# A two-layer diffusion backbone on one core: the MLPs' second product by seven quadrant products instead of eight

## The chip, the cores and the metric

The kernel runs on one core of a Trainium2 chip. The metric is the device time of one execution in microseconds (us). TensorE (PE in the profile) multiplies, ScalarE is ACT, VectorE is DVE, GpSimd is POOL, and SyncE (SP) issues the loads.

## The reference, cut to what matters

1024 sample tokens and 256 prompt tokens go through two layers with shared weights. Each layer is a mixer followed by an MLP; the change is mostly in the MLPs.

```
x = x + g1 * out                                   # mixer: layer 0 gMLP and retention, layer 1 pooling
h = _rms_norm(x, norm_mlp[i]) * (1.0 + sc2) + sh2
x = x + g2 * (jnp.square(jax.nn.relu(h @ mlp_w1[i])) @ mlp_w2[i])
```

The model width is 1024 and the hidden width 4096. In layer 0 a retention mixer also needs the running states of two scan directions at each of ten blocks of 128 tokens, and returns the prompt's final states.

## The kernel before, in words

All values are float32. For accuracy each operand of a product is kept as two tiles in a reduced format, a high part and the remainder (names ending in H and L), and each product is three matmuls: high x high, high x low, low x high (`pair_pass`, where nearly all matmuls have line L314). The high part is made by a copy on ScalarE, the low part by a subtraction: on GpSimd for weights (`split_lo`), on VectorE for the hidden values (`hidden_lo`).

Everything is transposed: the features are on the 128 partitions and the tokens run along the free axis in three blocks `TB`: two of 512 sample tokens, one of 256 prompt tokens. The sum `X` (8 tiles of features by 1280 tokens) stays in SBUF.

Each MLP runs over NCH = 16 chunks of 256 hidden features. One chunk has these steps:

- First product: six groups (three token blocks by two tiles of 128 hidden features), each of 8 x 3 = 24 matmuls, into PSUM banks 0 and 1 in turn.
- For each group: relu on ScalarE (L774), square on VectorE (L1336), high part on ScalarE into `midH` (L767), low part on VectorE into `midL` (L1329).
- Second product: 24 groups (three token blocks by eight tiles of output features), each of 2 x 3 = 6 matmuls, into banks 2 to 5 in turn. VectorE adds each one, times the gate, into `X` (L1061, called an eviction below). TensorE may use a bank again when the eviction four groups back is done.
- Weights: SP loads 1 MB of W1 or W2 into `stage`, ScalarE makes `ringH` (L532, `split_hi`), GpSimd makes `ringL` (L854, `split_lo`). There is one `stage`, and a ring of two slots: one holds W1 and one W2. W1 of the next chunk is split as soon as the last first-product group has been issued, W2 of this chunk when the chunk before is over.

The order on each engine is written out by hand, and semaphores (counts of finished steps) tie the engines together. Chunks 1 to 14 are a hardware loop with one body per engine, for each of the two layers. Layer 0's chunks carry extra work for layer 1's modulation: `ada_part` on VectorE in four parts of four instructions, and `ada_of_chunk` on TensorE.

The retention stage of layer 0 spills the states to DRAM and then reads them back block by block (`state_loads`), into two buffers per direction, `S[d][k % 2]`. The prompt's final states also lie in `S[d][0]`, and must have been written out before block 0 can be loaded there. GpSimd computes tables for the pooling mixer (`bandT`, `bandM` and others) just behind chunk 0 of layer 0.

## Time and profile before

| what | value |
|---|---|
| median of 3 runs | 2645.57 us (2644.88 to 2650.03) |
| the profiled execution | 2645.16 us, of which 2643.4 us are the profiled span |
| TensorE matmul busy | 2561.9 us, 97% of the span |
| VectorE busy | 1351.4 us, 51% |
| ScalarE busy | 593.9 us, 22% |
| GpSimd busy | 544.8 us, 21% |
| DMA | mean 75 GB/s |
| matmuls of the two MLPs | most of the rows of L314, which hold 83% of the chain that ended last |

A matmul's row is longer than the time in which it keeps the next one waiting, since matmuls are pipelined: what counts for TensorE is the distance from one start to the next. The same holds a little for VectorE and ScalarE, whose next instruction starts shortly before the row of the last one ends.

### The profile page before, as it was taken

What the parts mean: (1) busy time and instruction counts of PE and PEld (TensorE: products, weight loads), DVE (VectorE), ACT (ScalarE), POOL (GpSimd) and SP (SyncE); (2) the same over time, 40 slices, a digit from 0 to 9 for tenths busy, and PEclk for the clock granted to TensorE, in tenths of its full rate; (3) what the DMA queues carried; (4) which work ended last, traced back from release to release, by engine and by line L of the source; (5) the groups of instructions that cost most, each with busy time, mean ns of one, the idle gap of its engine ahead of it and who ended that gap; (6) DMA issues with size and microseconds to landing.
All of it is one profiled execution on the core that took longest, in us unless ns stands there. A gap on an engine that the chain in (4) does not pass through costs nothing.

```text
span 2643.4 us, 37530 instructions
## 1 busy us (share of the span) xinstructions
PE 2561.9 (97%) x14604; PEld 2240.7 (85%) x14604; DVE 1351.4 (51%) x2366; ACT 593.9 (22%) x982; POOL 544.8 (21%) x230
## 2 busy tenths in 40 slices
PE   7899999979999999999999999999999999999998
PEld 3878899977888888888888888888888888888887
DVE  6635752264385556554556555564444444444445
ACT  3311122142231111111111112751112111121112
POOL 6124321162121212111112111011121211212110
PEclk9999999989999999999999999899999999999999
DMA  7314523274212211211211211011010100101102
GB/s 236 149 67 142 166 96 112 95 265 168 72 33 80 71 56 56 95 56 56 71 56 56 95 56 32 25 32 33 32 48 32 48 32 32 48 32 48 32 32 80
DMA packets 126263, 199.48 MB, mean 75 GB/s; under 512 B 4420, under 2 KB 102504, under 8 KB 125800
## 3 DMA queue, kind: packets, MB, share of 16 engines
q1 hardware_dynamic: 123216, 188.76, 21.1%
q10 hardware_dynamic: 2968, 9.63, 1.2%
q8 instruction: 55, 0.90, 0.1%
q14 instruction: 24, 0.20, 0.0%
HBM read 167.44 MB, written 26.74 MB: 73 GB/s over the span
## 4 chain that ended last, share of the span: by engine, by line
PE 88%; DVE 5%; issue 2%; DMA 2%; ACT 2%; POOL 1%; ACTq 0%; SPq 0%; DVEq 0%; POOLq 0%
PE bank L314 83%; PE bank L1404 1%; PE bank L1432 1%; PE bank L1557 1%; DMA ada_st_in<-in_ada_w_dram 1%; PE bank L1469 1%; DVE ada_acc_in L1053 0%; PE bank L1735 0%; DVE vtok L1107 0%; DMA SB<-state_spill 0%; DVE xgm L1220 0%; POOL ringL L854 0%; DVE h1L L1227 0%; DVE X L1061 0%; ACT pF L736 0%
## 5 line engine op out<-in xcount | busy, mean ns | idle before, releaser
L854 POOL TENSOR_TENSOR ringL<-stage,ringH 128x2048 fp32r<-128x2048 f32 x82 | 392.8, 4790 | 1823.1 <-ACT ringH L532 1823.1
L1061 DVE SCALAR_TENSOR_TENSOR X<-bank,mod,X 128x512 f32<-128x512 f32 (+1 forms) x792 | 515.1, 660 | 363.4 <-PE bank L314 359.1
L314 PE MATMUL bank<-midH,ringH 128*128 128x512 f32 (+1 forms) x1536 | 546.7, 356 | 3.3 <-DVE X L1061 3.3
L314 PE MATMUL bank<-midL,ringH 128*128 128x512 f32 (+1 forms) x1536 | 544.9, 355 | 0.0
L314 PE MATMUL bank<-midH,ringL 128*128 128x512 f32 (+1 forms) x1536 | 544.7, 355 | 0.0
L314 PE MATMUL bank<-hH,ringH 128*128 128x512 f32 (+1 forms) x1248 | 447.2, 358 | 0.2 <-DVE hL L1227 0.2
L314 PE MATMUL bank<-hH,ringL 128*128 128x512 f32 (+1 forms) x1248 | 442.5, 355 | 0.0
L314 PE MATMUL bank<-hL,ringH 128*128 128x512 f32 (+1 forms) x1248 | 442.4, 355 | 0.0
L1336 DVE TENSOR_TENSOR relu<-relu 128x512 f32<-128x512 f32 (+1 forms) x192 | 146.3, 763 | 568.9 <-ACT relu L774 568.8
L774 ACT ACTIVATE relu<-bank 128x512 f32<-128x512 f32 (+1 forms) x192 | 100.9, 527 | 1375.9 <-PE bank L314 1375.9
L314 PEld LDWEIGHTS bank<-midH,ringH 128*128 128x128 f32 x1536 | 291.5, 190 | 46.1 <-DVE X L1061 6.5
L314 PEld LDWEIGHTS bank<-midH,ringL 128*128 128x128 f32 x1536 | 291.2, 190 | 40.6
L314 PEld LDWEIGHTS bank<-midL,ringH 128*128 128x128 f32 x1536 | 291.7, 190 | 39.5
L314 PE MATMUL bank<-h1H,ringH 128*128 128x512 f32 (+1 forms) x768 | 272.4, 355 | 0.2 <-DVE h1L L1227 0.2
L314 PE MATMUL bank<-h1L,ringH 128*128 128x512 f32 (+1 forms) x768 | 271.8, 354 | 0.0
L314 PE MATMUL bank<-h1H,ringL 128*128 128x512 f32 (+1 forms) x768 | 271.6, 354 | 0.0
L314 PEld LDWEIGHTS bank<-hH,ringL 128*128 128x128 f32 x1248 | 236.6, 190 | 33.4
L314 PEld LDWEIGHTS bank<-hH,ringH 128*128 128x128 f32 x1248 | 236.9, 190 | 32.5 <-DVE hL L1227 1.0
L314 PEld LDWEIGHTS bank<-hL,ringH 128*128 128x128 f32 x1248 | 236.9, 190 | 31.5
L314 PE MATMUL bank<-ringH,hH 128*128 128x256 f32 x640 | 186.2, 291 | 13.7 <-DVE hL L1030 13.7
L314 PE MATMUL bank<-ringL,hH 128*128 128x256 f32 x640 | 183.3, 286 | 0.0
L314 PE MATMUL bank<-ringH,hL 128*128 128x256 f32 x640 | 183.1, 286 | 0.0
(191 smaller groups left out, 2888.1 us busy)
## 6 DMA issues: line engine op xcount, KB each, us to landing
stage<-in_mlp_w_dram SPq DMA_DIRECT2D x64, 1024.0 KB, 5.3
ada_st_mlp<-in_ada_w_dram SPq DMA_DIRECT2D x18, 1536.0 KB, 8.3
stage<-in_ev_w_in_dram SPq DMA_DIRECT2D x14, 1024.0 KB, 5.1
ada_st_in<-in_ada_w_dram SPq DMA_DIRECT2D x8, 1536.0 KB, 9.5
ada<-in_ada_w_dram SPq DMA_DIRECT2D x8, 1024.0 KB, 13.3
x_spill<-X SPq DMA_DIRECT2D x1, 5120.0 KB, 18.5
gate_spill<-gate_st ACTq DMA_DIRECT2D x8, 640.0 KB, 3.7
gt<-gate_spill SPq DMA_DIRECT2D x20, 256.0 KB, 3.3
```

The costliest lines, as they stand in the source:

```text
L314: mm = nc.tensor.matmul(out, a, b, start=first and n == 0, stop=last and n == 2)
L774: nc.scalar.activation(r_b[g % 3][:, 0:w], bank[g if first and g < 4 else g % 2][:, 0:w], ACT.Relu).then_inc(relu_ok[l], 1)
L854: nc.gpsimd.tensor_tensor(ringL[slot][:, :], stage[:, :], ringH[slot][:, :].bitcast(F32), ALU.subtract).then_inc(w_lo, 1)
L1061: V.scalar_tensor_tensor(out=X[:, d, cols(t)], in0=src[:, 0:TB[t][1]], scalar=gate_ap, in1=X[:, d, cols(t)], op0=ALU.mult, op1=ALU.add).th ...
L1336: V.tensor_tensor(r, r, r, ALU.mult).then_inc(sqr_ok[l], 1)
L1404: mm = nc.tensor.matmul(ADA_BANK[:, col(4 * j + 2 * i)], ada_acc[pr][:, j, i, :], ones[:, 0:2], start=True, stop=True)
L1432: mm = nc.tensor.matmul(bank[i // 2][0:2, UC * (i % 2):UC * (i % 2 + 1)], sc2[:, k, :], ada0[i][:, k, :], start=(k == 0), stop=(k == DT - 1))
L1469: mm = nc.tensor.matmul(bank[6 + d][:, h * P:(h + 1) * P], kx[j % 2][:, d, h, :], val[:, n, h * P:(h + 1) * P], start=True, stop=True)
L1557: mm = nc.tensor.transpose(tile_pair(q, j)[:, d * P:(d + 1) * P], X[:, d, n * P:(n + 1) * P], ident)
```

## The change

Three things change.

First, in chunks 1 to 14 of both layers the second product of the 1024 sample tokens is cut in quadrants: two halves of hidden features (A11, A12, A21, A22 are W2's quadrants) and two halves of tokens (B11, B12, B21, B22 are the hidden values'). Eight products of quadrants become seven, of sums S1 to S4 of weights and T1 to T4 of hidden values (the scheme of Strassen and Winograd). Products 1, 6, 7, 4 run on in one bank without clearing it, and 5 and 3 likewise, so each of the 28 results (seven products by four tiles) is added to one tile of `X`. The weight sums are made on GpSimd, the T sums on VectorE, and both are split in high and low parts. The eight prompt groups stay as they are. `mlp_fast` is the loop body on each engine.

Second, `state_loads` uses the other buffer, `S[d][(k + 1) % 2]`, so block 0's load no longer waits for the final states to have left; the wait for the last input product moves behind the second state loads, the gate loads and a weight load.

Third, the pooling tables are computed in layer 0's last chunk rather than behind its first. Some small tiles move (`r_b`, `fin`).

```diff
+FACTORS = {1: ("A11", "B11"), 2: ("A12", "B21"), 3: ("S4", "B22"), 4: ("A22", "T4"), 5: ("S1", "T1"), 6: ("S2", "T2"),
+           7: ("S3", "T3")}
+GOES_TO = {1: (0, 0), 2: (0, 0), 6: (0, 1), 5: (1, 1), 7: (1, 1), 3: (0, 1), 4: (1, 0)}
+CHAIN = {6: 1, 7: 6, 4: 7, 3: 5}
+FAST_SEQ = ([(1, d) for d in range(HD)] + [(2, d) for d in range(HD)]
+            + [(p, d) for d0 in range(0, HD, 2) for p in (6, 5, 7, 3, 4) for d in (d0, d0 + 1)] + [("prompt", d) for d in range(DT)])
+FAST_BANK = [(2, 3, 6, 1, 4, 5, 2, 3)[d] if p == "prompt" else (6, 1)[d % 2] if p in (2, 3, 5) else 2 + d for p, d in FAST_SEQ]
+LO_ORDER = ["B11", "B21", "T1", "T2", "T3", "B22", "T4", "p0", "p1"]
...
-        sp.wait_ge(in_mm, IN_CUM[N_IN])
-        sp.wait_ge(a_spilled[0], 16 * 2 * NTB * HT)
-        sp.wait_ge(a_spilled[1], 16 * 2 * NTB * HT)
-
...
-                sp.dma_start(S[d][k % 2][:, :, :].rearrange("p h e -> p (h e)"), s_dram[d][k]).then_inc(s_back[k % 2], 16)
+                sp.dma_start(S[d][(k + 1) % 2][:, :, :].rearrange("p h e -> p (h e)"), s_dram[d][k]).then_inc(s_back[k % 2], 16)
```

The end of the new body on ScalarE (the last line makes W1's high part):

```diff
+            relu(4, hidden("p0")[2])
+            square(4, hidden("p0")[2])
+            act.wait_ge(sqr_ok[l], n0 + 5)
+            high("p0")
+            relu(5, hidden("p1")[2])
+            square(5, hidden("p1")[2])
+            act.wait_ge(sqr_ok[l], n0 + 6)
+            high("p1")
+            split_hi(U + 2, (m1_mm[l], n0 + PAIRS), U_MLP[l] % 2)
```

The new body on GpSimd:

```diff
+        def mlp_fast(l, ch):
...
+            pool.wait_ge(w_raw, 16 * (U + 2))
+            pool.wait_ge(m2_mm[l], products(l, ch) - DT)
+            nc.gpsimd.tensor_tensor(s1, a21, a22, ALU.add).then_inc(s_add[l], 1)
+            nc.gpsimd.tensor_tensor(s3, a11, a21, ALU.subtract).then_inc(s_add[l], 1)
+            pool.wait_ge(s_add[l], 4 * ch - 3)
+            nc.gpsimd.tensor_tensor(s2, s1, a11, ALU.subtract).then_inc(s_add[l], 1)
+            pool.wait_ge(s_add[l], 4 * ch - 1)
+            nc.gpsimd.tensor_tensor(s4, a12, s2, ALU.subtract).then_inc(s_add[l], 1)
+            split_lo(U + 1, (U_MLP[l] + 1) % 2)
+            pool.wait_ge(s_hi[l], ch)
+            pool.wait_ge(t_full[l], 4 * ch - 3)
+            nc.gpsimd.tensor_tensor(sumL[:, :, :], sumF[:, :, :], sumH[:, :, :].bitcast(F32), ALU.subtract).then_inc(s_lo[l], 1)
+            split_lo(U + 2, U_MLP[l] % 2)
```

The new body on VectorE, where `evict(n)` is one eviction and `lower` makes a low part:

```diff
+        def mlp_fast(l, ch):
...
+            ada(0)
+            square(0)
+            lower("B11", b11)
+            ada(1)
+            square(1)
+            lower("B21", b21)
+            square(2)
+            dve.wait_ge(sqr_ok[l], n0 + 3)
+            V.tensor_tensor(t1, b12, b11, ALU.subtract).then_inc(t_full[l], 1)
+            for n in range(2 * HD):
+                evict(n)
+            ada(2)
+            ada(3)
+            dve.wait_ge(sqr_ok[l], n0 + 4)
...
+            for n in range(2 * HD, FAST_GRP):
+                evict(n)
+                if n in (11, 13):
+                    lower("p0" if n == 11 else "p1")
```

The new body on TensorE (each `second_product` first waits until the last eviction from its bank is done):

```diff
+        def mlp_fast(l, ch):
...
+            first_product(0)
+            pe.wait_ge(m2_ev[l], p0 - 4)
+            first_product(1)
+            pe.wait_ge(relu_ok[l], n0 + 1)
+            first_product(2)
+            pe.wait_ge(w_lo, UA + 2)
+            for n in range(HD):
+                second_product(n)
+            pe.wait_ge(relu_ok[l], n0 + 2)
+            for n in range(HD, 2 * HD):
+                second_product(n)
...
+            first_product(3)
+            pe.wait_ge(m2_ev[l], p0 + 2 * HD)
+            first_product(4)
+            pe.wait_ge(relu_ok[l], n0 + 4)
+            first_product(5)
+            pe.wait_ge(s_lo[l], ch)
+            pe.wait_ge(relu_ok[l], n0 + 5)
+            for n in range(2 * HD, 7 * HD):
+                second_product(n)
```

The body that GpSimd runs for each of chunks 1 to 14 of layer 1 was, before (`ringL_56` and `ringL_57` are the low parts of W2 and of the next chunk's W1):

```order
L986 ISA
L854 TENSOR_TENSOR ringL_56<-stage,ringH_54 128x2048 [waits w_hi]
L853 REGISTER_ALU
L854 TENSOR_TENSOR ringL_57<-stage,ringH_55 128x2048 [waits w_hi]
L986 REGISTER_ALU
L986 COMPARE_AND_BRANCH
```

and is now:

```order
L1096 TENSOR_TENSOR sumF<-stage 128x512 [waits m2_mm1]
L1097 TENSOR_TENSOR sumF<-stage 128x512
L1098 ISA
L1099 TENSOR_TENSOR sumF<-sumF,stage 128x512 [waits s_add1]
L1100 REGISTER_ALU
L1101 TENSOR_TENSOR sumF<-stage,sumF 128x512 [waits s_add1]
L967 TENSOR_TENSOR ringL_56<-stage,ringH_54 128x2048 [waits w_hi]
L1105 TENSOR_TENSOR sumL<-sumF,sumH 128x2048 [waits t_full1,s_hi1]
L966 REGISTER_ALU
L967 TENSOR_TENSOR ringL_57<-stage,ringH_55 128x2048 [waits w_hi]
```

Four sums stand ahead of the two splits, and the split of the sums stands between them. The last row, the next chunk's W1, stays last.

On VectorE, layer 1's body had all six low parts ahead of the first eviction; its rows at that place were, before:

```order
L1336 TENSOR_TENSOR relu_174<-relu_174 128x256 [waits relu_ok1]
L1329 TENSOR_TENSOR midL<-relu_173,midH 128x256 [waits mid_hi1]
L1329 TENSOR_TENSOR midL<-relu_174,midH 128x256 [waits mid_hi1]
L1058 ISA
L119 REGISTER_ALU [waits m2_mm1]
L1061 SCALAR_TENSOR_TENSOR X<-bank,mod,X 128x512 [waits m2_ev1]
```

and behind the low part of T4 (first row) it now has, where `bank1` is banks 2 and 3, `bank3` bank 6 and `bank0` bank 1:

```order
L1504 TENSOR_TENSOR ts4L_145<-relu0_178,ts4H_144 128x512 [waits mid_hi1]
L1194 REGISTER_ALU
L1197 SCALAR_TENSOR_TENSOR X_51<-bank1,mod_156,X_51 128x512 [waits m2_ev1,m2_mm1]
...
L1197 SCALAR_TENSOR_TENSOR X_51<-bank3,mod_156,X_51 128x512 [waits m2_ev1,m2_mm1]
L1197 SCALAR_TENSOR_TENSOR X_51<-bank0,mod_156,X_51 128x512 [waits m2_ev1,m2_mm1]
L1503 REGISTER_ALU
L1504 TENSOR_TENSOR midL_53<-midF_143,midH_52 128x256 [waits mid_hi1]
L1194 REGISTER_ALU
L1197 SCALAR_TENSOR_TENSOR X_51<-bank1,mod_156,X_51 128x512 [waits m2_ev1,m2_mm1]
```

The prompt's two low parts (rows with 128x256) have moved in between evictions: the first stands behind the fourth eviction of this phase and ahead of the fifth (that of product 7), the second two evictions later.

## Rows read from the trace of the kernel before

**Rows 1.** The page: span, busy time of TensorE's two parts and the others.

```profile
span 2643.4 us, 37530 instructions
PE 2561.9 (97%) x14604; PEld 2240.7 (85%) x14604; DVE 1351.4 (51%) x2366; ACT 593.9 (22%) x982; POOL 544.8 (21%) x230
```

**Rows 2.** Windows of one chunk: stretch, length, busy us by engine, granted clock, DMA.

```profile
1908.16:1963.24 55.08, 55.08 (x291) 47.55 (x290) 23.50 (x37) 9.58 (x14) 9.23 (x2) 1.00 0.12 38
...
1025.30:1081.80 56.50, 56.50 (x301) 48.81 (x300) 31.20 (x52) 9.58 (x14) 9.53 (x2) 1.00 0.19 65
```

**Rows 3.** Timeline of TensorE, layer 1: start, length, instruction (11 and 19 left out).

```profile
1850.17 0.28 PE L314 MATMUL bank<-midH,ringH 128*128 128x256 f32 x1
...
1852.57 0.28 PE L314 MATMUL bank<-midH,ringL 128*128 128x256 f32 x1
...
1855.12 0.39 PE L314 MATMUL bank<-h1H,ringH 128*128 128x512 f32 x1
...
1857.84 0.39 PE L314 MATMUL bank<-h1H,ringH 128*128 128x512 f32 x1
```

**Rows 4.** Timeline of ScalarE in one chunk of layer 1.

```profile
1968.95 0.60 ACT L774 ACTIVATE relu<-bank 128x512 f32<-128x512 f32 x1 [29.98 <-PE bank L314]
...
1990.95 0.38 ACT L774 ACTIVATE relu<-bank 128x256 f32<-128x256 f32 x1 [1.98 <-PE bank L314]
1991.23 0.41 ACT L767 ACTIVATE midH<-relu 128x256 fp32r<-128x256 f32 x1
1991.83 0.42 ACT L767 ACTIVATE midH<-relu 128x256 fp32r<-128x256 f32 x1 [0.19 <-DVE relu L1336]
1992.15 1.90 ACT L532 ACTIVATE ringH<-stage 128x2048 fp32r<-128x2048 f32 x1
```

**Rows 5.** Timeline of VectorE: square, eviction, five evictions in a row.

```profile
1914.51 0.69 DVE L1336 TENSOR_TENSOR relu<-relu 128x512 f32<-128x512 f32 x1 [5.69 <-ACT relu L774]
...
1940.07 0.75 DVE L1061 SCALAR_TENSOR_TENSOR X<-bank,mod,X 128x512 f32<-128x512 f32 x1 [0.61 <-PE bank L314]
...
1053.82 3.38 DVE L1061 SCALAR_TENSOR_TENSOR X<-bank,mod,X 128x512 f32<-128x512 f32 x5
```

**Rows 6.** Timelines of GpSimd and VectorE where they overlap.

```profile
1590.93 4.58 POOL L854 TENSOR_TENSOR ringL<-stage,ringH 128x2048 fp32r<-128x2048 f32 x1 [23.77 <-ACT ringH L532]
...
1591.97 3.82 DVE L1336 TENSOR_TENSOR relu<-relu 128x256 f32<-128x256 f32 x1 [2.46 <-ACT relu L774]
...
1589.09 0.42 DVE L1336 TENSOR_TENSOR relu<-relu 128x256 f32<-128x256 f32 x1 [2.81 <-ACT relu L774]
...
1939.05 4.62 POOL L854 TENSOR_TENSOR ringL<-stage,ringH 128x2048 fp32r<-128x2048 f32 x1 [18.08 <-ACT ringH L532]
...
1053.45 4.94 POOL L854 TENSOR_TENSOR ringL<-stage,ringH 128x2048 fp32r<-128x2048 f32 x1 [20.35 <-ACT ringH L532]
```

**Rows 7.** Timeline and windows: two stalls of TensorE and the stretches behind them.

```profile
1619.77 0.58 PE L314 MATMUL bank<-midH,ringH 128*128 128x256 f32 x1 [2.26 <-DVE X L1061]
...
1619.30:1622.60 3.30, 2.83 (x13) 2.83 (x14) 2.07 (x6) 0.00 (x0) 3.30 (x1) 0.51 0.01 2
...
563.00:568.00 5.00, 3.29 (x30) 3.10 (x30) 4.56 (x17) 3.37 (x10) 4.34 (x5) 1.00 0.65 190
```

**Rows 8.** Chain of waits and timeline at the start of the retention stage.

```profile
528.87 4.52 DMA out_dram<-SB
533.85 2.89 DMA SB<-state_spill
...
536.78 0.80 PE L1622 MATMUL bank<-val,pt 128*128 128x128 f32 x2 [5.86 <-DMA SB<-state_spill]
...
532.57 2.48 DVE L1175 TENSOR_TENSOR pt<-bank,tab 128x512 f32<-128x512 f32 x4 [11.49 <-DMA gate_spill<-gate_st]
```

**Rows 9.** Timeline of GpSimd: first and last table instruction, two 512-column products.

```profile
774.72 0.69 POOL L945 MEMSET bandT<- 128x144 f32 x4
...
785.25 0.10 POOL L972 MEMSET band_edge<- 128x1 f32 x1
...
542.60 2.49 POOL L919 TENSOR_TENSOR qd<-qk,tab 128x512 f32<-128x512 f32 x2 [9.11 <-PE bank L1623]
```

More of the change, by code:

```diff
@@ L221, in build @@
     ones = small("ones", [P, P])
-    r_b = [at(f"relu{i}", A_V + 2 * i, [P, 512]) for i in range(3)]
+    r_b = [at(f"relu{i}", A_AD + 3 + 2 * i, [P, 512]) for i in range(3)]
     acc = at("acc", A_E + 15, [P, T])
@@ L305, in cols, with pair_pass @@
         return slice(t0, t0 + w)
-    def pair_pass(out, w_hi_ap, w_lo_ap, m_hi_ap, m_lo_ap, first, last, weights_moving=False):
+    def pair_pass(out, w_hi_ap, w_lo_ap, m_hi_ap, m_lo_ap, first, last, weights_moving=False, chained=False):
         if weights_moving:
@@ L313, in pair_pass @@
         for n, (a, b) in enumerate(terms):
-            mm = nc.tensor.matmul(out, a, b, start=first and n == 0, stop=last and n == 2)
+            mm = nc.tensor.matmul(out, a, b, start=first and n == 0, stop=last and n == 2, skip_group_check=chained)
         return mm
@@ L348, in h_part, with hidden, weight @@
         return (hH, hL)[part][:, d, cols(tb)]
+    MID_PART = {"B11": (0, 0), "B21": (1, 0), "T1": (0, 1), "B22": (1, 1), "T2": (0, 0), "T3": (1, 0), "p0": (0, 2), "p1": (1, 2)}
+    def hidden(name):
+        if name == "T4":
+            return ts4H[:, :], ts4L[:, :], r_b[0][:, :]
+        k, tb = MID_PART[name]
+        return tuple(m[:, k, cols(tb)] for m in (midH, midL, midF))
+    def weight(l, name, d):
+        if name[0] == "S":
+            i = int(name[1]) - 1
+            return tuple(m[:, i, d * P:(d + 1) * P] for m in (sumH, sumL))
+        k, n0 = int(name[2]) - 1, HD * (int(name[1]) - 1)
+        return tuple(r[(U_MLP[l] + 1) % 2][:, k * D + (n0 + d) * P:k * D + (n0 + d + 1) * P] for r in (ringH, ringL))
     def slot_free(U):
@@ L477, in _ @@
         state_loads(0)
+        for d in range(2):
+            sp.dma_start(new_state[0, 0, d].rearrange("h d e -> d h e"), S[d][NT % 2][:, :, :]).then_inc(new_out, 16)
+        sp.wait_ge(new_out, 32)
         state_loads(1)
@@ L1357, in mlp, with square, lower, evict @@
                         finish(j)
+        def mlp_fast(l, ch):
+            n0, h0, p0 = PAIRS * ch, halves(l, ch), products(l, ch)
+            def square(g):
+                dve.wait_ge(relu_ok[l], n0 + g + 1)
+                V.tensor_tensor(r_b[g][:, :], r_b[g][:, :], r_b[g][:, :], ALU.mult).then_inc(sqr_ok[l], 1)
+            def lower(name, src=None):
+                hi, lo, full = hidden(name)
+                dve.wait_ge(mid_hi[l], h0 + LO_ORDER.index(name) + 1)
+                V.tensor_tensor(lo, full if src is None else src, hi.bitcast(F32), ALU.subtract).then_inc(mid_lo[l], 1)
+            def evict(n):
+                t, d = FAST_TILE[n]
+                own = earlier(FAST_TILE, n)
+                update(m2_mm[l], p0 + n + 1, m2_ev[l], bank[FAST_BANK[n]], mod[:, l, 5 * DT + d, TB[t][2]:TB[t][2] + 1], t, d,
+                       (m2_ev[l], p0 + own + 1))
+            def ada(part):
+                if l == 0:
+                    ada_part(BATCHES_L0 + ch, 1, part, 4)
+            b11, b21, b12 = (r[:, :] for r in r_b)
+            t1, t2, t3, t4, b22 = (hidden(name)[2] for name in ("T1", "T2", "T3", "T4", "B22"))
+            ada(0)
[12 more added lines that the diff above has]
+            dve.wait_ge(sqr_ok[l], n0 + 4)
+            dve.wait_ge(t_full[l], 4 * ch - 3)
+            V.tensor_tensor(t2, b22, t1, ALU.subtract).then_inc(t_full[l], 1)
+            V.tensor_tensor(t3, b22, b12, ALU.subtract).then_inc(t_full[l], 1)
+            dve.wait_ge(t_full[l], 4 * ch - 2)
+            V.tensor_tensor(t4, b21, t2, ALU.subtract).then_inc(t_full[l], 1)
+            lower("T1")
+            dve.wait_ge(t_full[l], 4 * ch)
+            lower("T2")
+            lower("T3")
+            lower("B22")
+            lower("T4")
+            for n in range(2 * HD, FAST_GRP):
+                evict(n)
+                if n in (11, 13):
+                    lower("p0" if n == 11 else "p1")
         mlp(0, 0, first=True)
@@ L1622, in _ @@
                         nc.tensor.matmul(out, pt[n % 2][:, d, h, :], val[:, n, h * P:(h + 1) * P], start=True, stop=False)
-                        mm = nc.tensor.matmul(out, qd[n % 2][:, d, h, :], S[d][n % 2][:, h, :], start=False, stop=True)
+                        mm = nc.tensor.matmul(out, qd[n % 2][:, d, h, :], S[d][(n + 1) % 2][:, h, :], start=False, stop=True)
                     mm.then_inc(y_mm, 1)
@@ L1658, in mlp @@
                     g = HT * nth + f
-                    after(pe, relu_ok[l], g - 3 if first else n0 + g - 1)
+                    after(pe, relu_ok[l], g - 3 if first else n0 + (max(g - 1, 0) if last else g - 1))
+                    if last and g == 1:
+                        pe.wait_ge(m2_ev[l], products(l, ch))
                     if first and g == HT:
```

214 lines of the change are left out of this document (156 added, 58 removed).

## The prediction

> **What bounds the kernel now.** I began with the page's busy times: TensorE is busy for 97% of the span, no other engine for more than 51% [rows 1]. The windows of single chunks sharpen that: in a chunk of layer 1 TensorE is busy for all of 55.08 us, in one of layer 0 for all of 56.50 us [rows 2]. A busy row is pipelined, so I took the distance between starts from the timeline: twelve 512-column matmuls lie between 1855.12 and 1857.84, or 0.2267 us each, and twenty 256-column ones between 1850.17 and 1852.57, or 0.12 us each [rows 3]. A chunk has 192 and 96 of them: 192 x 0.2267 + 96 x 0.12 = 55.04 us. So the MLP loops are bound by the sheer number of matmuls, and every other engine hides. The reader is to see both sides of this: each matmul taken out is worth its whole slot, and each wait put before TensorE costs its whole length.
>
> **What the change removes.** One product of eight, four tiles by three matmuls: 12 matmuls a chunk, 12 x 0.2267 = 2.72 us, in 28 chunks 76.2 us. That is all that can be won here. TensorE's own work per chunk of layer 1 falls to 52.32 us. (The page "TensorE: Matmul & The Clock Gate" of the Trainium skill, section "Back-to-back issue gap", would put a lone 512-column matmul's slot at about 216 ns; by that the saving would be 72.5 us. The trace has the duration, so the trace's is used.)
>
> **What it adds, step by step, for one chunk of layer 1.** C is the start of the chunk's first matmul. Durations: a group of the first product takes 24 slots, 5.44 us at 512 columns and 2.88 at 256; one tile of a quadrant product 3 slots, 0.68 us. An engine that waits for TensorE starts about 0.3 us after the last slot (a row is 0.39 long in a slot of 0.227, and the semaphore follows) [rows 3]. A relu or a high part takes 0.60 us, a VectorE operation of 512 columns from SBUF 0.69 (the next can start 0.61 after it) [rows 4, 5]. An eviction takes 0.75 alone; five in a row took 3.38, so each costs (3.38 - 0.75) / 4 = 0.66 when they queue [rows 5]. ScalarE's new squares I take like its copies.
>
> (a) *The first eight tiles.* Products 1 and 2 follow the third group. That ends at C + 16.32. Its relu, its square and T1 end near C + 18.5, and only then does VectorE evict, since T1 stands ahead. Four evictions for product 1 at 0.66 bring it to C + 21.2 for the first tile of product 2, which is out at C + 21.95. Product 2 has two banks (6 and 1) for four tiles, so its third tile, which could go at C + 16.32 + 6 x 0.68 = C + 20.4, waits until C + 22.0: a stall of 1.6 us. Before, four banks in turn and 1.36 us per group hid every eviction.
>
> (b) *The twenty tiles.* Groups four to six then end at C + 34.56. VectorE's T sums and low parts fit: from the fourth group's square at C + 30.4 eight operations of 0.61 end at C + 35.3, when the first of the twenty tiles comes. From there TensorE gives a tile every 0.68 us and VectorE takes one in 0.66, so it has nothing to spare: any block of VectorE goes to TensorE.
>
> (c) *The block.* ScalarE's last relu starts at C + 34.85; square, high part and then W1's high part follow as in its rows now, at about 0.4, 0.85 and 1.15 us behind it, so W1's high part runs from C + 36.0 to C + 37.9 and GpSimd's `split_lo` of W1 from C + 38.0 to C + 42.6 [rows 4, 6]. VectorE evicts tiles at C + 35.5, 36.2, 36.9 and 37.6 and comes to the prompt's first low part at C + 38.25. What a VectorE operation does that meets GpSimd's is in the trace: a 256-column square that takes 0.42 us alone took 3.82 when it came 1.04 us after the start of such a split, and ended 0.28 us after the split's end (1591.97 + 3.82 against 1590.93 + 4.58) [rows 6]. It did not run slower, it was held until the split was over. Evictions, which read PSUM and one tile of SBUF, aren't held: the one at 1940.07 took its usual 0.75 within the split of 1939.05 [rows 5, 6]. The low part has two SBUF inputs like the square, and stands in the middle of evictions. So VectorE stands from C + 38.25 to C + 42.6, then does the low part (0.34) and the eviction of product 7's first tile, out at C + 43.65. Product 4's first tile runs on in that bank and could have started at C + 34.56 + 8 x 0.68 = C + 40.0. Stall: 3.65 us. The Trainium skill's page "SBUF — State Buffer", section "Who interferes with whom", has this as a rule against such a placing: GpSimd and a VectorE operation with two SBUF inputs share an exclusive port, and whichever issued first holds the other for its whole instruction. By that rule too it hangs on who is first, by 0.25 us here.
>
> (d) *The clock.* A stall of 2.26 us before 1619.77 was followed by 3.3 us at a granted clock of 0.51, the 1.2 GHz level; from 563 to 568 TensorE stood for 1.71 of 5.00 us and the clock stayed at 1.00 [rows 7]. A stall of 3.65 us can bring such a stretch, whose cost is at most half of 3.3, 1.65 us, and nothing when VectorE's backlog holds TensorE anyway. Bounds 0 and 1.65 a chunk; I take the middle, 0.8.
>
> Sum per chunk: -2.72 + 1.6 + 3.65 + 0.8 = +3.33 us. Layer 0's chunks have the same order; TensorE's modulation sums (1.4 us) move to the chunk's start and shift everything together, and VectorE's `ada` parts lie in its idle stretches (C + 24 to C + 30 takes two of 2.1 us). So 28 x 3.33 = +93.2 us.
>
> **Edits costed at nothing.** GpSimd's four sums at 1.25 us each [rows 9] start when the prompt groups of the chunk before do, eight groups of 0.72 us, and are over near C; W2's low part then ends at C + 6.9 and is wanted at C + 16.3; the sums' low part follows T1, C + 18.7 to C + 23.3, wanted at C + 34.6. If that cover were gone, each would show at full length. VectorE evicts in that time, and isn't held. ScalarE's 1.9 us for the sums' high part ends near C + 4, before its first relu. The tables take 785.35 - 774.72 = 10.6 us of GpSimd [rows 9]; in the last chunk they lie between C + 7 and C + 18, and TensorE asks for them 20 us later. They may hold a square for about 1 us, where TensorE has two banks of slack.
>
> **The states.** At 528.87 the final states went out (4.52 us), then block 0's came in (2.89), and TensorE started at 536.78 [rows 8]. Now block 0 loads before that, and the last to be ready is VectorE's `pt`, which waits for a spill of the gates until 532.57 and has its first half after two of four operations, at 533.85 [rows 8]. The stage starts 2.9 us earlier, and what follows hangs on that start. Bounds: 0, if a later load takes it back, and 2.9. I take 2.9.
>
> The profiled execution took 2645.2 us, 0.4 below the median shown: 2645.2 + 93.2 - 2.9 = 2735.5. I say 2735 us.
>
> **The rivals.** For the forecast, the first low part held in nearly every chunk, I give 0.60.
> *Second low part held instead* (0.18). If VectorE reaches the first low part before GpSimd starts (0.25 us decide; a split can be held too, the one at 1053.45 took 4.94 us instead of 4.6 [rows 6]), the second one, two evictions later at C + 39.9, is held until C + 42.6 or a little more. Then tiles twelve and fourteen of the twenty wait, 1.6 and 1.3 us. Per chunk -2.72 + 1.6 + 2.9 = +1.8, and up to 0.6 for the clock: 2645.2 - 2.9 + 28 x (1.8 to 2.4) = 2693 to 2710.
> *Every stall brings the slow clock* (0.05). The Trainium skill's page on TensorE's clock gate, section "HAM oscillation — how this bites in real kernels", describes a loop whose idle gap throttles it in each turn. In this kernel, worked out from the rows: 1.65 instead of 0.8 in all 28 chunks, +24 us, 2759.
> *Not held: faster* (0.15). If low part and split don't meet, because ScalarE makes W1's high part some 2.5 us later than I have it (the split must start after C + 40.5), or because this operation isn't held, only stall (a) is left: 28 x (-2.72 + 1.6) - 2.9 = -34, 2611 us. For it speaks that five evictions in a row keep up with TensorE; against it the held square, of the same kind and smaller than usual. If stall (a) too were hidden, 2645 - 76 - 3 = 2566.
> *No change* (0.02): only by several of these at once.
>
> **How the numbers follow.** The range takes in the forecast with the clock's two bounds, 2645.2 - 2.9 + 28 x (2.53 to 4.2) = 2713 to 2760, and the second low part's 2693, with some 8 us at each end for the steps of 0.05 us that are multiplied by 28: 2685 to 2770. That leaves out the faster cases. A measurement here tells about 0.2%, 5 us. Faster 0.15, within 0.2% 0.02, slower 0.83.
>
> **What would show it.** A window of one chunk of layer 1: some 58.6 us instead of 55.08. TensorE idle 1.6 us after six of the first eight tiles, and 3.65 before product 4, released by an eviction. A VectorE row of the low part, 256 columns, of over 4 us, ending with a GpSimd `ringL` row. Slices of TensorE's clock below full in the MLP loops. The first retention matmul near 534. The prediction is wrong if that low part takes 0.4 us.

## The result: slower by 4.3%, and the profile after

The changed kernel takes 2761.2 us (median of 4 runs, 2754.2 to 2765.4), against 2645.5 us (4 runs, 2644.9 to 2650.0) for the kernel before: a ratio of 1.0431 with a 95% interval of 1.0406 to 1.0455, or 115.7 us more. The forecast was 2735 us with a range of 2685 to 2770. So the direction and the range held, and the forecast was 26 us too low.

The page of the changed kernel, in the parts that answer to [rows 1]; the third line gives each engine's share of the chain that ended last, the last is a group of instructions (line, operation, tiles, count, then busy us and mean ns, and the idle time before them):

```profile
span 2763.6 us, 39603 instructions
PE 2551.5 (92%) x14268; PEld 2208.3 (80%) x14268; DVE 1798.1 (65%) x2814; ACT 747.0 (27%) x1178; POOL 812.3 (29%) x370
PE 77%; DVE 9%; issue 9%; ACT 2%; DMA 1%; POOL 1%; DVEq 1%; ACTq 0%; SPq 0%; POOLq 0%
L1504 DVE TENSOR_TENSOR midL<-midF,midH 128x512 fp32r<-128x512 f32 x168 | 209.5, 1288 | 0.0
```

There are 336 matmuls fewer, yet TensorE's busy share fell from 97 to 92%, and its share of the chain from 88 to 77%; VectorE's rose from 5 to 9%. The last line names the place: low parts of hidden values, which take 0.41 us at 256 columns and 0.68 at 512, average 1.29. Some of them must be far longer.

The lengths of the chunks come from GpSimd's first sum, once in each chunk. Its second and last rows in the loops of layer 0 and of layer 1 (each pair spans twelve chunks; left out is the first interval of each loop, which is longer, 67.65 and 64.42 us):

```profile
845.30 1.29 POOL L1096 TENSOR_TENSOR sumF<-stage 128x512 f32<-128x512 f32 x1 [10.99 <-PE bank L362]
...
1574.09 1.30 POOL L1096 TENSOR_TENSOR sumF<-stage 128x512 f32<-128x512 f32 x1 [11.21 <-PE bank L362]
...
1906.66 1.30 POOL L1096 TENSOR_TENSOR sumF<-stage 128x512 f32<-128x512 f32 x1 [11.22 <-PE bank L362]
...
2623.45 1.29 POOL L1096 TENSOR_TENSOR sumF<-stage 128x512 f32<-128x512 f32 x1 [11.14 <-PE bank L362]
```

That is 728.79 / 12 = 60.73 us a chunk in layer 0 and 716.79 / 12 = 59.73 us in layer 1, against 56.50 and 55.08 before [rows 2]: 4.23 and 4.65 us more, or 14 x 8.88 = 124.3 us for the loops. At the start of the retention stage the changed kernel's trace is 5.7 us ahead (below). 124.3 - 5.7 = 118.6; the two profiled spans differ by 120.2.

VectorE in one chunk of layer 1. The bracket is the idle time before a row and what ended it:

```profile
1990.95 4.04 DVE L1197 SCALAR_TENSOR_TENSOR X<-bank,mod,X 128x512 f32<-128x512 f32 x6
1995.38 1.44 DVE L1197 SCALAR_TENSOR_TENSOR X<-bank,mod,X 128x512 f32<-128x512 f32 x2 [0.40 <-PE bank L362]
...
2007.97 2.80 DVE L1197 SCALAR_TENSOR_TENSOR X<-bank,mod,X 128x512 f32<-128x512 f32 x4 [0.15 <-PE bank L362]
2010.69 4.58 DVE L1504 TENSOR_TENSOR midL<-midF,midH 128x256 fp32r<-128x256 f32 x1
2015.20 1.40 DVE L1197 SCALAR_TENSOR_TENSOR X<-bank,mod,X 128x512 f32<-128x512 f32 x2
2016.52 0.41 DVE L1504 TENSOR_TENSOR midL<-midF,midH 128x256 fp32r<-128x256 f32 x1
```

GpSimd beside it:

```profile
1991.17 4.58 POOL L1105 TENSOR_TENSOR sumL<-sumF,sumH 128x2048 fp32r<-128x2048 f32 x1 [11.92 <-DVE midF L1526]
...
2010.45 4.54 POOL L967 TENSOR_TENSOR ringL<-stage,ringH 128x2048 fp32r<-128x2048 f32 x1 [14.70 <-ACT ringH L596]
```

The two low parts (128x256) are the same work. The second takes 0.41 us; the first takes 4.58 us, starts 0.24 us behind the split of W1, and ends 0.28 us behind the split's end (2015.27 against 2014.99). Apart from their place in the order the rows show no other difference. Evictions beside a GpSimd instruction of the same length do not grow: six of the first eight, most of them beside `sumL`, take 4.04 us, 0.67 each.

TensorE's two stalls in this chunk, and the second stall of the next chunk with what follows it:

```profile
1994.38 0.50 PE L362 MATMUL bank<-midH,ringH 128*128 128x512 f32 x1 [1.35 <-DVE X L1197]
2016.07 0.79 PE L362 MATMUL bank<-ts4H,ringH 128*128 128x512 f32 x1 [3.36 <-DVE X L1197]
...
2075.32 0.79 PE L362 MATMUL bank<-ts4H,ringH 128*128 128x512 f32 x1 [3.37 <-DVE X L1197]
2075.91 0.63 PE L362 MATMUL bank<-ts4L,ringH 128*128 128x512 f32 x1
2076.34 0.63 PE L362 MATMUL bank<-ts4H,ringL 128*128 128x512 f32 x1
```

Idle time in the bracket is counted from the end of the matmul before, whose row is 0.39 long in a slot of 0.227, so each stall costs 0.16 us more than it says: 1.52 and 3.52 us. The second is the start of product 4 (`ts4H`), released by the eviction behind the held low part. The matmuls behind it start 0.43 us apart instead of 0.227.

Windows of the changed kernel, columns as in [rows 2]; the granted clock stands behind the five busy times. The first two are neighbouring chunks of layer 1, the third is one of layer 0; the others begin at the end of the second stall, in the first chunk and in the next:

```profile
1972.47:2031.70 59.23, 54.51 (x279) 46.26 (x278) 37.16 (x52) 15.05 (x21) 18.83 (x7) 0.97 0.10 35
2031.70:2091.97 60.27, 55.55 (x279) 46.99 (x278) 37.31 (x52) 15.06 (x21) 18.85 (x7) 0.94 0.11 35
...
1089.79:1149.03 59.24, 54.52 (x291) 46.33 (x290) 48.46 (x69) 15.06 (x21) 18.84 (x8) 1.00 0.18 62
...
2016.00:2019.40 3.40, 3.33 (x8) 2.66 (x9) 3.28 (x6) 0.00 (x0) 0.00 (x0) 0.50 0.78 281
2019.40:2022.80 3.40, 3.40 (x17) 2.79 (x16) 3.22 (x6) 0.00 (x0) 0.00 (x0) 1.00 0.07 28
...
2074.60:2078.00 3.40, 2.68 (x6) 2.15 (x7) 3.40 (x6) 0.00 (x0) 0.00 (x0) 0.50 0.67 224
2078.00:2081.40 3.40, 3.40 (x10) 2.66 (x9) 2.22 (x4) 0.00 (x0) 0.00 (x0) 0.58 0.21 84
```

Right behind the stall the clock is at 0.50, the 1.2 GHz level: 8 matmuls start in 3.40 us where 15 start in the next 3.4 (the row counts two more, which began before it). Eight would need 8 x 0.2267 = 1.81 us, so by the starts alone the stretch costs 1.59 us; against a chunk without one it is 1.4, as worked out under (d) below. In the following chunk the low stretch is twice as long, 6.8 us, though its first 1.3 us still lie in the stall. In layer 1 the two lengths take turns, and so do the chunks, 59.2 and 60.27 us: the long stretch costs 1.05 us more. In layer 0 two of the twelve chunks have no low stretch, such as the third row's of 59.24 us. The whole kernel's mean granted clock is 0.967, against 0.988 before.

The start of the retention stage after the change, from the timelines of VectorE and TensorE, and the issue of the gates' last spill, for which `pt` waits, before and after:

```profile
528.86 0.38 ACTq L659 DMA_DIRECT2D gate_spill<-gate_st  x1
...
527.02 0.33 ACTq L723 DMA_DIRECT2D gate_spill<-gate_st  x1
...
530.33 2.48 DVE L1311 TENSOR_TENSOR pt<-bank,tab 128x512 f32<-128x512 f32 x4 [11.09 <-DMA gate_spill<-gate_st]
...
531.12 0.71 PE L1812 MATMUL bank<-val,pt 128*128 128x128 f32 x2 [2.03 <-issue]
```

It was 536.78 [rows 8] and is 531.12, 5.7 us earlier. Of this, 1.8 us are no effect of the states: the spill itself was issued that much earlier in this execution, behind work that the change does not touch (in the trace of the first experiment, whose program is the same up to there, it was issued at 529.12). The rest, 3.8 us, is the change's. TensorE no longer waits for a transfer of the states; it comes 0.79 us behind the first of four `pt` operations.

### The profile page after: what moved, and what is told of

It is laid out like the page before. It is cut to its first block, busy times and chain, and to the rows that moved or that the text cites. A ratio compares the mean times of both kernels' runs of the same rounds, so it can differ in the third digit from the quotient of the medians.

```text
span 2763.6 us, 39603 instructions
## 1 busy us (share of the span) xinstructions
PE 2551.5 (92%) x14268; PEld 2208.3 (80%) x14268; DVE 1798.1 (65%) x2814; ACT 747.0 (27%) x1178; POOL 812.3 (29%) x370
## 4 chain that ended last, share of the span: by engine, by line
PE 77%; DVE 9%; issue 9%; ACT 2%; DMA 1%; POOL 1%; DVEq 1%; ACTq 0%; SPq 0%; POOLq 0%
PE bank L362 72%; DVE X L1197 3%; PE bank L1594 1%; PE bank L1622 1%; PE bank L1747 1%; DVE relu L1499 1%; DMA ada_st_in<-in_ada_w_dram 1%; ACT relu L868 1%; PE bank L1659 1%; DVE ada_acc_in L1189 0%; PE bank L1987 0%; DVE vtok L1243 0%; DVE ada_acc_mlp L1189 0%; DVE xgm L1356 0%; POOL ringL L967 0%
## 5 line engine op out<-in xcount | busy, mean ns | idle before, releaser
L1197 DVE SCALAR_TENSOR_TENSOR X<-bank,mod,X 128x512 f32<-128x512 f32 (+1 forms) x1128 | 727.0, 684 | 179.9 <-PE bank L362 176.2
L596 ACT ACTIVATE ringH<-stage 128x2048 fp32r<-128x2048 f32 x82 | 156.6, 1909 | 691.2 <-PE bank L362 691.2
L362 PE MATMUL bank<-midH,ringH 128*128 128x256 f32 (+1 forms) x864 | 287.2, 332 | 43.0 <-DVE X L1197 43.0
L362 PE MATMUL bank<-midH,ringL 128*128 128x256 f32 (+1 forms) x864 | 282.9, 327 | 0.0
L362 PE MATMUL bank<-midL,ringH 128*128 128x256 f32 (+1 forms) x864 | 282.8, 327 | 0.0
L1105 POOL TENSOR_TENSOR sumL<-sumF,sumH 128x2048 fp32r<-128x2048 f32 x28 | 128.4, 4585 | 352.8 <-DVE midF L1526 352.8
L362 PEld LDWEIGHTS bank<-midH,ringH 128*128 128x128 f32 x864 | 164.5, 190 | 72.2 <-DVE X L1197 56.0
L1504 DVE TENSOR_TENSOR midL<-midF,midH 128x512 fp32r<-128x512 f32 x168 | 209.5, 1288 | 0.0
L1189 DVE SCALAR_TENSOR_TENSOR ada_acc_mlp<-ada_st_mlp,sc,ada_acc_mlp 128x384 f32<-128x384 f32 (+1 forms) x266 | 202.1, 823 | 0.0
L362 PE MATMUL bank<-midH,sumH 128*128 128x512 f32 x448 | 187.8, 419 | 0.0
```

Source lines behind the costliest of these rows:

```text
L362: mm = nc.tensor.matmul(out, a, b, start=first and n == 0, stop=last and n == 2, skip_group_check=chained)
L596: nc.scalar.activation(ringH[slot][:, :], stage[:, :], ACT.Copy).then_inc(w_hi, 1)
L1105: nc.gpsimd.tensor_tensor(sumL[:, :, :], sumF[:, :, :], sumH[:, :, :].bitcast(F32), ALU.subtract).then_inc(s_lo[l], 1)
L1189: V.scalar_tensor_tensor(out=acc, in0=src, scalar=sc2[:, k, cond:cond + 1], in1=acc, op0=ALU.mult, op1=ALU.add).then_inc(a_acc, 1)
L1197: V.scalar_tensor_tensor(out=X[:, d, cols(t)], in0=src[:, 0:TB[t][1]], scalar=gate_ap, in1=X[:, d, cols(t)], op0=ALU.mult, op1=ALU.add).th ...
L1504: V.tensor_tensor(lo, full if src is None else src, hi.bitcast(F32), ALU.subtract).then_inc(mid_lo[l], 1)
```

## The experiments

All edits are to the changed kernel, except where it says otherwise. Two theories stood: the forecast's, that GpSimd's split holds the prompt's first low part for its whole length and that the clock's fall comes on top; and its rivals, that VectorE simply has too much to do among the twenty tiles, and that the clock costs nothing because VectorE's backlog holds TensorE anyway.

**Both low parts ahead of the split.** Same instructions, another place on VectorE.

```diff
-                if n in (11, 13):
-                    lower("p0" if n == 11 else "p1")
+                if n in (8, 9):
+                    lower("p0" if n == 8 else "p1")
```

> The prompt's two low parts stand right behind the first and second of the twenty evictions instead of the fourth and sixth, so both come before GpSimd starts W1's split. Theory (held port): neither is held, the 3.5 us stall before product 4 and the slow clock behind it are gone, a chunk of layer 1 takes 53.9 us (52.3 of matmuls and 1.6 of stall before product 2's third tile), the kernel 2645.5 - 5.5 - 28 x 1.15 = 2608 us. Rival (VectorE's 28 evictions are the bound, the low part is only where it shows): a chunk stays at 57 or more, the kernel above 2700 us.

Measured: 2608.7 us (2606.8 to 2619.9), ratio to the kernel before 0.9861 (0.9838 to 0.9883), chunks of 54.00 and 55.40 us. VectorE at the place that mattered, and GpSimd:

```profile
1985.92 0.42 DVE L1504 TENSOR_TENSOR midL<-midF,midH 128x256 fp32r<-128x256 f32 x1
...
1986.91 0.41 DVE L1504 TENSOR_TENSOR midL<-midF,midH 128x256 fp32r<-128x256 f32 x1
1987.24 5.35 DVE L1197 SCALAR_TENSOR_TENSOR X<-bank,mod,X 128x512 f32<-128x512 f32 x8
```

```profile
1987.72 4.62 POOL L967 TENSOR_TENSOR ringL<-stage,ringH 128x2048 fp32r<-128x2048 f32 x1 [14.66 <-ACT ringH L596]
```

The same two low parts take 0.42 and 0.41 us, and eight evictions that run across the whole split take 0.67 each. The work on VectorE is unchanged, so it was not too much; it was in the wrong place. Where two instructions of 0.4 us stand in a chunk was worth 152 us (2761.2 - 2608.7), more than the 115.7 that the whole change cost.

**The split behind both low parts.** The other end of the same meeting: VectorE's order stays, GpSimd waits.

```diff
+            pool.wait_ge(mid_lo[l], halves(l, ch) + FAST_MID)
             split_lo(U + 2, U_MLP[l] % 2)
```

> The order on VectorE stays, but GpSimd's split of W1 waits until the prompt's second low part is done. Theory (held port): the low parts take 0.42 us, the split starts near C + 40.5, a chunk of layer 1 takes 53.9 us, the kernel 2608 us, as when the low parts are moved. Rival (the low part waits for something else, such as ScalarE's high part): its row stays over 4 us and the kernel at 2760 us.

Measured: 2612.3 us (2610.6 to 2620.4), ratio 0.9887 (0.9860 to 0.9914). Low parts of 0.42 and 0.41 us again, with the split starting 0.16 us behind the end of the second. It does not matter which of the two moves. TensorE keeps only the stall of the first eight tiles:

```profile
2016.43 0.50 PE L362 MATMUL bank<-midH,ringH 128*128 128x512 f32 x1 [1.35 <-DVE X L1198]
```

**The split in four pieces.** Same work on GpSimd in the same place, as four instructions of 512 columns. It asks for how long the port is held.

```diff
-            split_lo(U + 2, U_MLP[l] % 2)
+            slot = U_MLP[l] % 2
+            pool.wait_ge(w_hi, U + 3)
+            for i in range(4):
+                s = slice(512 * i, 512 * (i + 1))
+                e = nc.gpsimd.tensor_tensor(ringL[slot][:, s], stage[:, s], ringH[slot][:, s].bitcast(F32), ALU.subtract)
+            e.then_inc(w_lo, 1)
```

> GpSimd's split of W1 in four instructions of 512 columns instead of one of 2048, nothing else. Theory (the port is held for one instruction): each low part waits for at most one piece, 1.25 us; stalls of TensorE sum to about 3.1 us with the one before product 2, a chunk of layer 1 takes 55.5 us, the clock stays at full, the kernel 2645.5 - 5.5 + 28 x 0.4 = 2651 us. Rival (GpSimd keeps the port as long as it has instructions ready): the low part is held for over 4 us still, the kernel at 2760 us.

Measured: 2656.7 us (2651.3 to 2659.2), ratio 1.0042 (1.0031 to 1.0054), chunks of 55.6 and 56.96 us. VectorE's two low parts, then GpSimd's four pieces:

```profile
2009.57 1.33 DVE L1509 TENSOR_TENSOR midL<-midF,midH 128x256 fp32r<-128x256 f32 x1
...
2012.14 1.43 DVE L1509 TENSOR_TENSOR midL<-midF,midH 128x256 fp32r<-128x256 f32 x1
```

```profile
2009.33 5.40 POOL L1110 TENSOR_TENSOR ringL<-stage,ringH 128x512 fp32r<-128x512 f32 x4 [14.67 <-ACT ringH L596]
```

A low part now waits for one piece, 1.33 us in all instead of 4.58, and gets in between two pieces that lie back to back. The second, untouched before, now meets a piece too and takes 1.43. So the hold lasts for one instruction, not for GpSimd's whole piece of work. The four pieces take 5.40 us where one instruction takes 4.6. Product 4 now starts only 0.27 us late, and a stall of 1.04 us (0.88 by the profile's idle time) comes five us later, behind the second low part. With the first stall, TensorE stands for 2.8 us a chunk, where 3.1 were expected, and no low stretch of the clock is left in the loops.

**TensorE kept busy in the stall.** This one weighs the clock by itself. Fifteen matmuls, whose results nothing reads, stand ahead of product 4's first tile, where TensorE otherwise stands still: 420 matmuls more in the kernel. The wait for the last relu moves ahead of them, since they write bank 0.

```diff
             for n in range(2 * HD, 7 * HD):
+                if n == 4 * HD:
+                    pe.wait_ge(relu_ok[l], n0 + 6)
+                    wH, _ = weight(l, "A22", 0)
+                    mH, _, _ = hidden("B22")
+                    for _ in range(15):
+                        nc.tensor.matmul(bank[0][:, :], wH, mH, start=True, stop=True)
                 second_product(n)
```

> TensorE's stall before product 4 is filled with 15 matmuls of 512 columns (3.4 us) into bank 0, whose results nothing reads; 420 matmuls more in all. Theory (about 50 us of the loss are the 1.2 GHz stretches behind the stall): the clock stays at 2.4 GHz, a chunk of layer 1 takes 57.6 us instead of 59.7, the kernel 2645.5 - 5.5 + 28 x 2.55 = 2711 us. Rival (only the stalls count, the clock is hidden behind VectorE's backlog): 2761 us or more.

Measured: 2721.4 us (2718.4 to 2722.6), ratio 1.0286 (1.0262 to 1.0310), mean granted clock 0.989. TensorE at the place, and the window of one chunk:

```profile
1991.05 0.39 PE L362 MATMUL bank<-midH,sumL 128*128 128x512 f32 x1
1991.28 3.56 PE L1951 MATMUL bank<-midH,ringH 128*128 128x512 f32 x15
1994.86 0.49 PE L362 MATMUL bank<-ts4H,ringH 128*128 128x512 f32 x1
1995.19 0.40 PE L362 MATMUL bank<-ts4L,ringH 128*128 128x512 f32 x1
...
2003.55:2061.41 57.86, 56.48 (x294) 47.80 (x293) 36.58 (x54) 15.05 (x21) 18.89 (x7) 1.00 0.10 36
```

Product 4 starts 3.81 us after the last matmul of product 7, as before (3.36 + 0.39 = 3.75), but its matmuls now follow at 0.23 us instead of 0.43. The wait is the same and the kernel is 40 us faster with more to compute: the chunks are 57.9 us instead of 59.73 in layer 1 and 59.27 instead of 60.73 in layer 0. So the low clock cost at least 1.8 and 1.5 us a chunk; at least, since the filling has a small cost of its own (product 4 comes 0.06 us later, for one). It did not hide behind VectorE's backlog. The kernel's 2721.4 us are 10 above the expectation: its chunk of layer 1 was put at 57.6 us and took 57.9, by a cost that no term of the forecast has (see the sum at the end).

**Evictions ahead of T1.** VectorE evicts six of the first eight tiles before the third square and T1 (before: square, T1, then all eight; one of layer 0's `ada` parts moves ahead as well).

```diff
-            square(2)
-            dve.wait_ge(sqr_ok[l], n0 + 3)
-            V.tensor_tensor(t1, b12, b11, ALU.subtract).then_inc(t_full[l], 1)
-            for n in range(2 * HD):
-                evict(n)
             ada(2)
+            for n in range(6):
+                evict(n)
+            square(2)
+            dve.wait_ge(sqr_ok[l], n0 + 3)
+            V.tensor_tensor(t1, b12, b11, ALU.subtract).then_inc(t_full[l], 1)
+            for n in range(6, 2 * HD):
+                evict(n)
             ada(3)
```

> Only step (a) is mended: VectorE evicts six of the first eight tiles ahead of the third square and of T1 (in layer 0 one of the four modulation parts moves ahead of them). Theory: TensorE's stall before product 2's third tile falls from 1.5 to 0.4 us, everything else stays, the held low part and the slow clock too: 28 x 1.2 = 33 us less than the changed kernel, 2728 us. Rival (the 1.2 GHz stretches depend on where in the chunk the stall falls, so that the saving is lost or doubled): anything from 2710 to 2761 us.

Measured: 2717.6 us (2711.2 to 2719.5), ratio 1.0273 (1.0256 to 1.0290). TensorE's two stalls in a chunk of layer 1, and the window of the next chunk:

```profile
1964.32 0.50 PE L362 MATMUL bank<-midH,ringH 128*128 128x512 f32 x1 [0.17 <-DVE X L1197]
...
1986.02 0.49 PE L362 MATMUL bank<-ts4H,ringH 128*128 128x512 f32 x1 [3.37 <-DVE X L1197]
...
1996.18:2054.28 58.10, 54.57 (x279) 46.22 (x278) 37.03 (x54) 15.05 (x21) 18.87 (x8) 0.97 0.10 36
```

The first stall falls from 1.35 to 0.17 us as expected, the second stays. The gain, 43.6 us, is 10 more than the expected 28 x 1.2, so the rival has some truth: the low stretches changed too. In layer 1 every chunk now has a low stretch of 3.4 us and none of 6.8 us, and in layer 0 seven of twelve chunks (58.1 to 58.2 us) have no low stretch, where the changed kernel had two (59.2 us). With the stall at the same length and the same place of the program, only the shorter stall ahead of it and the chunk's length changed. Which of the two decides over the stretches is open.

**The second low part held.** The forecast's rival, made on purpose: the first low part goes ahead of the split, the second stays.

```diff
-                if n in (11, 13):
-                    lower("p0" if n == 11 else "p1")
+                if n in (8, 13):
+                    lower("p0" if n == 8 else "p1")
```

> The prompt's first low part behind the first eviction, the second left where it is, so that only the second meets the split. Theory: the first takes 0.42 us, the second is held for about 3 us, TensorE stalls 0.9 and 1.3 us later in the phase (each tile after waits for an eviction four back), a chunk of layer 1 takes 56.1 us and one of layer 0 57.6, the clock mostly stays; the kernel 2645.5 - 5.5 + 28 x 1.06 = 2670 us, up to 2685 with some slow stretches. Rival (the hold costs the same wherever it falls): 2740 us or more.

Measured: 2676.0 us (2672.1 to 2678.3), ratio 1.0116 (1.0100 to 1.0131), chunks of 56.25 and 57.6 us. VectorE's second low part and TensorE's stalls:

```profile
2022.29 3.08 DVE L1504 TENSOR_TENSOR midL<-midF,midH 128x256 fp32r<-128x256 f32 x1
```

```profile
2026.08 0.50 PE L362 MATMUL bank<-midH,sumH 128*128 128x512 f32 x1 [0.64 <-DVE X L1197]
2028.71 0.50 PE L362 MATMUL bank<-midH,sumH 128*128 128x512 f32 x1 [0.95 <-DVE X L1197]
...
1920.73:1976.97 56.24, 53.29 (x279) 44.95 (x278) 34.96 (x54) 15.06 (x21) 18.91 (x8) 1.00 0.12 37
```

Held for 2.7 us instead of 4.2, two stalls of 0.64 and 0.95 us instead of one of 3.36, and a clock that stays at 1.00. That is 85 us less than the changed kernel for an instruction moved by three places.

**The states alone.** The kernel before with only the second part of the change: the other buffer for the block states, the final states written out behind the first loads, the wait for the last input product behind the second state loads.

```diff
-                sp.dma_start(S[d][k % 2][:, :, :].rearrange("p h e -> p (h e)"), s_dram[d][k]).then_inc(s_back[k % 2], 16)
+                sp.dma_start(S[d][(k + 1) % 2][:, :, :].rearrange("p h e -> p (h e)"), s_dram[d][k]).then_inc(s_back[k % 2], 16)
```

> The kernel before with the change of the states alone: other buffer, block 0's load ahead of the final states' way out, the wait for the last input product later. Theory: the retention stage starts about 4 us earlier and keeps it: 2641 us, at most 2639.8. Rival (a later load or the slow clock takes it back): 2645 us.

Measured: 2640.8 us (11 runs, 2636.7 to 2646.9), ratio 0.9986 (0.9976 to 0.9996), 4.3 us less than the kernel before on the same chip (1.1 to 6.3 by the interval). The stage's start:

```profile
531.03 2.48 DVE L1174 TENSOR_TENSOR pt<-bank,tab 128x512 f32<-128x512 f32 x4 [11.10 <-DMA gate_spill<-gate_st]
...
531.82 0.46 PE L1621 MATMUL bank<-val,pt 128*128 128x128 f32 x2 [2.04 <-issue]
```

5.0 us earlier than before, of which 1.1 again lie ahead of the stage (the gates' spill was issued at 527.72, before at 528.86). The other 3.8 stand against the forecast's 2.9.

**Both cures together.** The low parts at 8 and 9 and the evictions ahead of T1.

> Both mended: low parts early as in e1, evictions ahead of T1 as in e5. Theory: a chunk of layer 1 takes 52.7 us and one of layer 0 54.2, against 55.08 and 56.53 before; the kernel 2608.7 - 28 x 1.2 = 2575 us. Rival (with the long stall gone, another wait of the same size takes its place in (a), such as the sums' low part or the T sums coming late): 2590 us or more.

Measured: 2582.3 us (5 runs, 2580.3 to 2588.8), ratio 0.9764 (0.9751 to 0.9778): 63 us less than the kernel before and 179 less than the changed one. Window of one chunk, and the only idle row of TensorE left in a chunk of layer 1:

```profile
1925.16:1977.99 52.83, 52.66 (x279) 45.16 (x278) 32.35 (x53) 15.05 (x21) 18.94 (x7) 1.00 0.12 40
```

```profile
1951.42 0.50 PE L362 MATMUL bank<-midH,ringH 128*128 128x512 f32 x1 [0.17 <-DVE X L1197]
```

TensorE is busy for 52.66 of 52.83 us, as it was for the whole chunk before the change. The chunks had been expected at 52.7 and 54.2 us. This chunk is 2.25 us shorter than the 55.08 of before, and one of layer 0 (54.33) 2.17 shorter than 56.50: 14 x 4.42 = 62 us, and with the states' 4.3 the sum is 66, where 63 was measured.

## Why the prediction was right in kind and 26 us short

**The saving.** 12 matmuls of 0.2267 us, 2.72 us a chunk, was right: TensorE's own work was put at 52.32 us, and the chunk with both cures takes 52.83, of which 0.33 is a rest of stall (a) and 0.11 the slow start behind it.

**(a) The stall of the first eight tiles.** 1.6 us forecast, 1.52 measured, at the place given (product 2's third tile), released by an eviction. Moving the evictions took it away and left the second alone.

**(b) VectorE without slack among the twenty tiles.** Right in its numbers: four evictions take 2.80 us, eight take 5.35, 0.67 to 0.70 each, and each engine follows the other. As a rival, "VectorE is simply too slow", it fell with the first experiment.

**(c) The block.** 3.65 us forecast, 3.52 measured. The chunk's sequence was forecast to 0.25 us between the split's start and the low part; it was 0.24, and in all 28 chunks it was the first low part that was held, for some 4.2 us. That the chain of estimates came out so near is in part luck: it has many terms rounded to 0.05 or 0.1 us, and 0.25 us decided between this case and a rival. The low part took 4.58 us. Experiments from both sides (low parts moved, split moved) and from the length of the hold (four pieces) show that it is this meeting, and that the hold lasts for GpSimd's one instruction. The Trainium skill says the same of the shared port in "SBUF — State Buffer", section "Who interferes with whom": exclusive, for the whole instruction, and with no effect on a VectorE operation that reads at most one tile from SBUF and runs in no two-port mode. Here the trace agrees, with 4.58 us for the low part and 0.67 for an eviction within a split.

One rival was left open by the experiments: that the kind of operation decides, since the low part is a TENSOR_TENSOR and the eviction a SCALAR_TENSOR_TENSOR. The changed kernel's trace settles it. In layer 0 the first of `ada_part`'s SCALAR_TENSOR_TENSORs with two SBUF tensors meets W2's split:

```profile
853.00 4.62 POOL L967 TENSOR_TENSOR ringL<-stage,ringH 128x2048 fp32r<-128x2048 f32 x1 [2.53 <-ACT ringH L596]
...
853.30 5.26 DVE L1189 SCALAR_TENSOR_TENSOR ada_acc_mlp<-ada_st_mlp,sc,ada_acc_mlp 128x384 f32<-128x384 f32 x2
```

The first of these two takes 4.73 us and the other its usual 0.61. So the same kind of operation is held with two inputs in SBUF, and not held as an eviction, with one of them in PSUM.

The rival in which the second low part is held instead did not happen, but made on purpose it gave 2676 us, where it had been put at 2693 to 2710: its stalls had been put at 1.6 and 1.3 us and measured 0.80 and 1.12 (0.64 and 0.95 with the 0.16 added), and they brought no low clock, for which it had allowed up to 0.6.

**(d) The clock.** This is the term that was mis-sized: "Bounds 0 and 1.65 a chunk; I take the middle, 0.8". What it cost shows against chunks with the same two stalls and no low stretch. In layer 0 the changed kernel has two of these itself, at 59.24 us (the window above), against 60.73 in the mean: 1.5 us. In layer 1 the filled stall gives 57.89 us in the mean, 0.06 of it the filling's, so 57.83 against 59.73: 1.9 us. By length, a stretch of 3.4 us costs 1.4 and one of 6.8 us 2.4. (The 1.59 from the starts alone is 0.2 too much: the first matmul behind the stall is slow at full clock too, and a short wait further on falls away.) The mean of both layers is 1.7, twice the forecast's 0.8.

The upper bound failed because it took the one stretch of 3.3 us as the longest. Stretches of 6.8 us came in every second chunk of layer 1 and in a third of layer 0's, and the trace of before already had one, at another place:

```profile
1660.40:1667.20 6.80, 6.28 (x29) 6.31 (x30) 2.67 (x5) 5.81 (x12) 2.71 (x4) 0.50 0.00 0
```

The middle failed because next to nothing pulled towards the lower bound: "nothing when VectorE's backlog holds TensorE anyway" was wrong, since at this clock TensorE makes a tile in 3 x 0.43 = 1.3 us while VectorE clears its backlog at 0.67. The rival "every stall brings the slow clock", 2759 us at a chance of 0.05, was nearly the result, in part by luck: its 1.65 a chunk is about the mean of 0, 1.4 and 2.4 us, none of which it named. The Trainium skill's page "TensorE: Matmul & The Clock Gate", section "HAM oscillation — how this bites in real kernels", had it as a loop that is throttled in each turn. The trace agrees in kind for layer 1, where each turn has a low stretch, and not wholly for layer 0, where in the chunks of 59.2 us it is missing.

**The states.** 2.9 us forecast, 3.8 measured at the stage's start in both kernels, and 4.3 by the medians. The mechanism was right: the transfer left the path and `pt` became the last to be ready. The size was off by two things. The forecast let TensorE start behind two of the four `pt` operations; it starts 0.79 us behind the start of the first, which is 0.5 us earlier. And `pt` starts 3.31 us behind the issue of the gates' spill (527.02 to 530.33) where it was 3.71 (528.86 to 532.57), 0.4 us less: the final states' way out no longer runs beside that spill. 2.9 + 0.5 + 0.4 = 3.8. That the two transfers slow each other is worked out from these times, not tried by itself.

**Edits costed at nothing.** The sums, their low part, W2's split and the tables cost nothing that can be found: with both stalls away, the chunk is at TensorE's own work. One effect was not foreseen and stays hidden: W2's split now holds an `ada` operation for 4.1 us in thirteen of layer 0's fourteen chunks (as at 853.30), and TensorE does not wait for it.

**The sum by measured terms.** A chunk of layer 1: -2.72 + 1.52 + 3.52 + 1.90 = 4.22; measured 4.65. The other 0.43 us has no term in the forecast, and a chunk without a low stretch has it too (59.24 - 56.50 = 2.74 in layer 0, where -2.72 + 1.52 + 3.52 is 2.32). Some 0.3 of it is the first matmul after a wait, which keeps the next one 0.33 us behind it instead of 0.23 (as from 1994.86 to 1995.19 behind the filled stall): in the filled kernel this comes three times a chunk, behind both stalls and once more four us on (2056.95 to 2057.28). The last 0.1 is not placed. Against the forecast's terms, for 28 chunks: the clock 1.7 instead of 0.8, +25 us; the 0.4 us without a term, +12; the two stalls 0.21 us shorter, -6; the states -1. That is +30 us. The profiled execution of 2765.4 us lies 30 above the forecast, though it was 1.8 us ahead before the retention stage; the median lies 26 above. The clock's term is the main error, the missing 0.4 us the second. The sign given for a chunk, "some 58.6 us", does not follow from the forecast's own sum, which gives 55.08 + 3.33 = 58.4.

## What to carry to other kernels

In a loop bound by TensorE, look for every VectorE instruction with two SBUF inputs that can meet a long GpSimd instruction, and ask what stands behind it: here two instructions of 0.4 us in the wrong place cost 152 us in all, and one line moved them. Where two engines run at 0.66 and 0.68 us a tile, the order between them matters more than the work saved. And cost a recurring stall of some 3.5 us on TensorE at its length plus a stretch at half clock, here 1.4 or 2.4 us, not at the middle between that and nothing, until a run with the stall filled shows otherwise.
